# One-pass spreading of the gate rows of the first block, with a high and a low part, and the bound's exponential taken after the spread

## The reference

```
log_f = log_sigmoid(f_pre);  b = cumsum(log_f);  inter = b + m
d     = b[t] - b[s] + i[s]                  (s <= t, else -inf)
m_t   = max(inter, max_s d)
w     = exp(d - m_t);  qk = (q . k) * w
h     = num / max(|den|, exp(-m_t))
```

## Time and profile before

| | |
|---|---|
| median of 3 runs | 1403.32 us (1402.62 to 1403.69) |
| the profiled execution | 1404.49 us |
| its span, from the first to the last instruction | 1402.7 us |
| TensorE busy | 1386.1 us (99%) |
| VectorE busy | 1121.9 us (80%) |
| ScalarE busy | 848.6 us (61%) |
| mean granted clock of TensorE | 0.998 |

### The profile page before, as it was taken

One profiled execution on the slowest core, in us unless ns is written; L12 is line 12 of the kernel. 1 busy time (PEld: TensorE's weight loads), 2 busy tenths in 40 slices (PEclk: granted clock), 3 DMA queues, 4 the chain that ended last, 5 costly groups with the idle time before them and its releaser, 6 DMA issues.

```text
span 1402.7 us, 25844 instructions
## 1 busy us (share of the span) xinstructions
PE 1386.1 (99%) x10437; PEld 1306.4 (93%) x10437; DVE 1121.9 (80%) x1700; ACT 848.6 (61%) x1315; POOL 101.4 (7%) x157
## 2 busy tenths in 40 slices
PE   8999999999999999999999999999999999999998
PEld 8898888899889888899999999998999999999987
DVE  7898988889898889888788788767687787876653
ACT  6776776345876875446577575544464864755442
POOL 2000111100000011103100000000031000000000
PEclk9999999999999999999999999999999999999999
DMA  9643999986545999978955588887699556878662
GB/s 262 166 143 102 285 270 277 293 230 177 143 141 151 298 273 284 295 217 245 314 155 155 172 238 239 241 247 219 181 260 310 151 151 180 238 215 232 187 184 72
DMA packets 472981, 301.34 MB, mean 215 GB/s; under 512 B 15116, under 2 KB 454416, under 8 KB 472736
## 3 DMA queue, kind: packets, MB, share of 16 engines
q1 hardware_dynamic: 455344, 239.57, 61.2%
q0 software_dynamic: 16704, 58.29, 12.7%
q10 hardware_dynamic: 816, 1.84, 0.4%
HBM read 289.43 MB, written 1.05 MB: 207 GB/s over the span
## 4 chain that ended last, share of the span: by engine, by line
PE 79%; DVE 12%; ACT 3%; issue 3%; DMA 2%; SPq 0%; DVEq 0%; ACTq 0%
PE acc L2122 13%; PE acc L2123 13%; PE acc L2124 13%; PE mx L2139 8%; PE acc L2139 6%; PE mx L2140 4%; DVE w_lo L1186 4%; PE acc L2140 3%; DVE ada_acc L1276 2%; PE mx L2123 2%; PE mx L2124 2%; PE mx L2122 2%; DMA raw<-in_w_in 1%; ACT w_hi L596 1%; PE acc L2167 1%
## 5 line engine op out<-in xcount | busy, mean ns | idle before, releaser
L1186 DVE TENSOR_TENSOR w_lo<-raw,w_hi 128x1024 fp32r<-128x1024 f32 x450 | 542.5, 1220 | 126.6 <-ACT w_hi L596 124.6
L596 ACT ACTIVATE w_hi<-raw 128x1024 fp32r<-128x1024 f32 x450 | 464.5, 1052 | 130.3 <-DMA raw<-in_w_in 61.4
L2122 PE MATMUL acc<-h,w_hi 128*128 128x256 f32 (+1 forms) x1472 | 418.9, 285 | 2.9 <-DVE w_lo L1186 1.9
L2123 PE MATMUL acc<-h,w_hi 128*128 128x256 f32 (+1 forms) x1472 | 413.0, 281 | 0.0
L2124 PE MATMUL acc<-h,w_lo 128*128 128x256 f32 (+1 forms) x1472 | 411.8, 280 | 0.0
L2122 PEld LDWEIGHTS acc<-h,w_hi 128*128 128x128 f32 x1472 | 277.4, 188 | 8.1 <-DVE w_lo L1186 2.3
L2123 PEld LDWEIGHTS acc<-h,w_hi 128*128 128x128 f32 x1472 | 277.6, 189 | 1.4 <-issue 1.0
L2124 PEld LDWEIGHTS acc<-h,w_lo 128*128 128x128 f32 x1472 | 278.0, 189 | 0.0
L2139 PE MATMUL mx<-u,w_hi 128*128 128x512 f32 x756 | 264.4, 392 | 0.0
L2140 PE MATMUL mx<-u,w_lo 128*128 128x256 f32 x756 | 213.1, 282 | 0.0
L2139 PEld LDWEIGHTS mx<-u,w_hi 128*128 128x128 f32 x756 | 141.9, 188 | 29.2
(11 more groups left out here) (339 smaller groups left out, 2297.7 us busy)
## 6 DMA issues: line engine op xcount, KB each, us to landing
raw<-in_w_in SPq DMA_DIRECT2D x132, 512.0 KB, 4.1
ada<-in_w_ada POOLq DMA_DIRECT2D x96, 512.0 KB, 5.9
raw<-in_w_ffn_in SPq DMA_DIRECT2D x88, 512.0 KB, 4.1
raw<-in_w_up SPq DMA_DIRECT2D x64, 512.0 KB, 5.5
raw<-in_w_down SPq DMA_DIRECT2D x64, 512.0 KB, 5.9
raw<-in_w_out SPq DMA_DIRECT2D x32, 512.0 KB, 3.9
raw<-in_w_ffn_out SPq DMA_DIRECT2D x32, 512.0 KB, 4.1
raw<-in_w_ret_o SPq DMA_DIRECT2D x16, 512.0 KB, 4.1
```

The source lines that it names most:

```text
L596: nc.scalar.activation(w_hi[:, n % NS], raw[:, n % NS], ACT.Copy).then_inc(hi_ready, 1)
L1186: V.tensor_tensor(w_lo[:, n % NS], raw[:, n % NS], w_hi[:, n % NS].bitcast(F32), ALU.subtract).then_inc(lo_ready, 1)
L2122: mm(outp, w_hi[:, i % NS, k], rhs[:, k, 0], start=k == 0, stop=False)
L2123: mm(outp, w_hi[:, i % NS, k], rhs[:, k, 1], start=False, stop=False)
```

## The change

1. `g_M` is split into a high part (fp32r) on partitions 0 to 3 and a low part on partitions 32 to 35 of a zeroed tile `g_M2` of 36 rows. The spreading matmul has 36 rows, a selecting column that is repeated over the 128 outputs (`pick`), and one pass in fp32r; it sums both parts. All four heads are done after slab 9.
2. The bound: G is clipped before the exponential (to the logarithms of the old limits), split in the same way (`g_G2`), spread in one pass, and ScalarE takes exp(-2 x) as it reads the spread rows from the bank. `forget_exp` and `gates_clipped` are gone.
3. `sums(0)` moves into slab 10, after its third piece. `gate_columns` goes from behind slab 9 to behind slab 10.
4. VectorE: slab 8 is read out before the splitting; `w_lo` of slabs 13 and 14 follows the last tap instead of preceding it; 2 memsets at the start of a layer, 4 small copies at the program's start for `pick` and `pick_pairs`.
5. ScalarE: `spread_exp` is ahead of the convolution's silu.
6. The padding ahead of `u2` grows from 32 to 148 words a partition, beside the new tiles.

```diff
+            with ExitStack() as until_values:
+                g_M2 = sb("g_M2", [36, S], F32R, until_values)
+                g_G2 = sb("g_G2", [36, S], F32R, until_values)
...
-                def forget_exp():
-                    act.wait_ge(f_G, l + 1)
-                    nc.scalar.activation(g_E[:], g_G[:], ACT.Exp, scale=-2.0).then_inc(f_E, 1)
...
-                    nc.scalar.activation(ebc[:], mx[:, 0], ACT.Copy).then_inc(f_bcsb, 1)
+                    nc.scalar.activation(ebc[:], mx[:, 0], ACT.Exp, scale=-2.0).then_inc(f_bcsb, 1)
...
                 ahead(13)
-                forget_exp()
                 ahead(14)
                 head_square(0)
                 head_seed(0)
                 ahead(15)
+                spread_exp()
                 conv_silu()
                 spread_max()
-                spread_exp()
...
+                boot.done(V.tensor_copy(pick[0:32], con[0:32, K_ID:K_ID + 4]))
+                boot.done(V.tensor_copy(pick[32:36], con[32:36, K_ID + 32:K_ID + 36]))
+                boot.done(V.tensor_copy(pick_pairs[0:32], con[0:32, K_ID:K_ID + 4].unsqueeze(2).to_broadcast([32, 4, HD])))
+                boot.done(V.tensor_copy(pick_pairs[32:36], con[32:36, K_ID + 32:K_ID + 36].unsqueeze(2).to_broadcast([4, 4, HD])))
...
-                    V.tensor_tensor(g_G[:], g_F[:], g_M[:], ALU.add).then_inc(f_G, 1)
-                    dve.wait_ge(f_G, l + 1)
-
-                def gates_clipped():
-                    dve.wait_ge(f_E, l + 1)
-                    V.tensor_scalar(g_E[:], g_E[:], 1e30, 1e-33, ALU.min, ALU.max).then_inc(f_E2, 1)
+
+                def gate_parts():
+
+                    c.link(V.tensor_copy(g_M2[0:4], g_M[:]))
+                    V.tensor_tensor(g_M2[32:36], g_M[:], g_M2[0:4].bitcast(F32), ALU.subtract).then_inc(f_parts, 1)
+
+                def bound_parts():
+
+                    c.link(V.tensor_tensor(g_G[:], g_F[:], g_M[:], ALU.add))
+                    c.link(V.tensor_scalar(g_G[:], g_G[:], G_HIGH, G_LOW, ALU.min, ALU.max))
+                    c.link(V.tensor_copy(g_G2[0:4], g_G[:]))
+                    V.tensor_tensor(g_G2[32:36], g_G[:], g_G2[0:4].bitcast(F32), ALU.subtract).then_inc(f_parts, 1)
...
                 c.done(V.memset(ones4[:], 1.0))
+                c.done(V.memset(g_M2[:].bitcast(F32), 0.0))
+                c.done(V.memset(g_G2[:].bitcast(F32), 0.0))
...
                 def gate_rows(n):
-                    pe.wait_ge(s_con, 32)
-                    pe.wait_ge(f_M, l + 1)
+                    pe.wait_ge(f_parts, l * 2 + 1)
...
-                        ins = mm(mx[:, 1 + n, i * S:(i + 1) * S], con[0:4, K_SEL + h * P:K_SEL + (h + 1) * P], g_M[:],
+                        ins = mm(mx[:, 1 + n, i * S:(i + 1) * S], pick[:, h:h + 1].to_broadcast([36, P]), g_M2[:],
...
-                        ins = mm(mx[:, 0, n * S:(n + 1) * S], con[0:4, K_PAIR + n * P:K_PAIR + (n + 1) * P], g_E[:],
-                                 start=True, stop=True)
+                        ins = mm(mx[:, 0, n * S:(n + 1) * S], pick_pairs[:, 2 * n:2 * n + 2].rearrange("p h d -> p (h d)"),
+                                 g_G2[:], start=True, stop=True)
```

More of the change, by code:

```diff
@@ L16 @@
+import math
 from contextlib import ExitStack
@@ L37 @@
 BIG = 1e30
+G_LOW, G_HIGH = -0.5 * math.log(1e30), -0.5 * math.log(1e-33)
 A_PROJ, A_OUT, A_MLP = 23, 8, 64
@@ L250, in program @@
         ada_part = sb("ada_part", [P, 4])
+        pick = sb("pick", [36, 4], F32R)
+        pick_pairs = sb("pick_pairs", [36, 4, HD], F32R)
         few = sb("few", [P, 16])
@@ L253, in program @@
         wgrp = sb("wgrp", [P, LAYERS * 4, P])
-        sb("before_u2", [P, 32])
+        sb("before_u2", [P, 148])
         with ExitStack() as mlp:
@@ L387, in program @@
         cv_first = sem("cv_first"); cv_ready = sem("cv_ready"); cv_silu = sem("cv_silu")
-        f_abs = sem("f_abs"); f_ln = sem("f_ln"); f_M = sem("f_M"); f_G = sem("f_G"); f_E = sem("f_E"); f_E2 = sem("f_E2")
+        f_abs = sem("f_abs"); f_ln = sem("f_ln"); f_M = sem("f_M");
         f_bc = sem("f_bc"); f_bcsb = sem("f_bcsb"); f_uc = sem("f_uc"); f_ucsb = sem("f_ucsb")
-        f_exp = sem("f_exp"); ml_v = sem("ml_v"); ml_rs = sem("ml_rs")
+        f_parts = sem("f_parts"); f_exp = sem("f_exp"); ml_v = sem("ml_v"); ml_rs = sem("ml_rs")
         ml_s = sem("ml_s"); ml_arg = sem("ml_arg"); ml_w = sem("ml_w"); ml_p = sem("ml_p"); ml_nd = sem("ml_nd")
@@ L1444, in arguments @@
                         dve.wait_ge(s_con, 32)
-                    dve.wait_ge(f_bcsb, l * 3 + h // 2 + 1)
+                    dve.wait_ge(f_bcsb, l * 3 + h // 2 + 2)
                     if h >= 2:
@@ L1469, in ml_bounded @@
                     dve.wait_ge(ml_d, l + 1)
-                    dve.wait_ge(f_bcsb, l * 3 + 3)
+                    dve.wait_ge(f_bcsb, l * 3 + 1)
                     c.link(V.tensor_tensor(m_d, m_d, ebc[:], ALU.max))
@@ L1567, in _ @@
                 gate_maxima()
-                to_sbuf(7)
+                to_sbuf(7, 8)
+                gate_parts()
                 convolve(2)
-                gates_clipped()
-                to_sbuf(8)
+                bound_parts()
+                lo_upto(p0 + 12)
+                convolve(3)
                 lo_upto(p0 + 14)
-                convolve(3)
                 gate_negated()
@@ L2233, in project @@
                              before=(lambda k: pe.wait_ge(h_ready, l * 16 + k + 1)) if i == 0 else
-                             (lambda k: norm_sum(l * 2) if k == (4 if l else 7) else None) if i == 1 else None).then_inc(slab_used, 1)
+                             (lambda k: norm_sum(l * 2) if k == (4 if l else 7) else None) if i == 1 else
+                             (lambda k: sums(0) if k == 3 else None) if i == 10 else None).then_inc(slab_used, 1)
                 def gate_rows(n):
-                    pe.wait_ge(s_con, 32)
-                    pe.wait_ge(f_M, l + 1)
+                    pe.wait_ge(f_parts, l * 2 + 1)
                     for i in range(2):
                         h = 2 * n + i
-                        ins = mm(mx[:, 1 + n, i * S:(i + 1) * S], con[0:4, K_SEL + h * P:K_SEL + (h + 1) * P], g_M[:],
+                        ins = mm(mx[:, 1 + n, i * S:(i + 1) * S], pick[:, h:h + 1].to_broadcast([36, P]), g_M2[:],
                                  start=True, stop=True)
@@ L2250, in gate_columns @@
                         mm(mx[:, 3, 4 * t:4 * t + 4], g_u[:, t * P:(t + 1) * P], con[0:4, K_ID:K_ID + 4], start=True, stop=True)
[L2251 removed]
+                    pe.wait_ge(f_parts, l * 2 + 2)
                     for n in range(2):
[L2253 to L2254 removed]
+                        ins = mm(mx[:, 0, n * S:(n + 1) * S], pick_pairs[:, 2 * n:2 * n + 2].rearrange("p h d -> p (h d)"),
+                                 g_G2[:], start=True, stop=True)
                     ins.then_inc(f_uc, 1)
@@ L2396, in _ @@
                     rest_of_vectors()
-                project(3, 4, 5, 6, 7, 8)
+                project(3, 4, 5, 6, 7, 8, 9)
                 gate_rows(0)
-                project(9)
-                sums(0)
+                gate_rows(1)
+                project(10)
                 gate_columns()
-                project(10)
-                gate_rows(1)
                 project(11, 12)
+                pe.wait_ge(f_bcsb, l * 3 + 2)
+                ml_scores(0)
                 pe.wait_ge(f_bcsb, l * 3 + 3)
-                ml_scores(0)
-                pe.wait_ge(f_bcsb, l * 3 + 2)
                 values(0)
```

1 line of the change is left out of this document (removed).

## The result

The changed kernel takes 1405.89 us (median of 20 runs, 1403.65 to 1409.14) beside 1403.61 us (20 runs, 1402.09 to 1405.51) for the kernel before on the same chip: a ratio of 1.0013 [1.0007, 1.0019], 1.8 us more by the ratio (2.3 by the two medians), where 1 us less was forecast. A second measurement gave 1.0010 [1.0002, 1.0019]. Small as it is, the sign is wrong, and the time lies above the range.

The account below looks back on a forecast made before the run. TensorE, 99% busy, was taken as the bound, tied to a chain of VectorE, sync queue and copies. Gains kept, 0.1 + 0.8, about 1 us, took the profiled 1404.49 to 1403.5, median 1402.3; range 1399.5 to 1405.3.

Parts of the forecast that it names:

- The slack: First layer, before slab 12: TensorE could begin at 51.98 but does at 54.36, so 2.4 us to draw on.
- new waits at slab 12: TensorE waits for VectorE's reading of slab 9: 2.6 us in the first layer, 1.3 in the second.
- Rival 2: TensorE's saving counts in full in both layers, 2.8 + 2.5 = 5.3 us, so 1398.0; chance 12%.
- rival 3: Gate rows still cost 1.0 us and more; TensorE only waits less at slab 12, time within 0.3; inside the 45%.
- The padding: Moved padding ahead of u2: costed at nothing, since no row showed an address mattering.
- Rival 1: New waits lower the clock at slabs 12 and 13, 1.7 us each: 1403.9 (27%, first layer) or 1405.2 (8%, both).
- Step 1: Four start copies add 0.7 us to VectorE, carried to slab 9; VectorE's 2.1 us delay ends in idle before 60.24.
- The term of the memsets: Two memsets lie where VectorE waits for the norm's sum and cost nothing; without that cover, 0.4 us.
- Step 2: Result of sums(0), counted from slab 8's end: equally late in the first layer, 0.26 us later in the second.
- TensorE's sum: Small matmuls per layer: gate rows 0.47, sums(0) 1.17, gate_columns 0.92, together 2.56 instead of 5.08; saves 2.5 us.
- Step 3: VectorE's added less removed work: net +1.44 us a layer, range 1.2 to 1.7.
- the place that counts: Copies of pair 1 on the sync queue set the end; forecast 0.1 us earlier in the first layer, 0.8 in the second.

Follow-up runs that it names:

- sums_first: Changed kernel with sums(0) right behind slab 9, ahead of the gate rows, instead of inside slab 10; 1405.22 us, ratio to the kernel before 1.0005.
- start_twice: Changed kernel with its four start copies done twice at the same place; 1406.55 us, ratio to the kernel before 1.0025.
- sums_late: Changed kernel with sums(0) after slab 10's seventh piece instead of its third; 1406.64 us, ratio to the kernel before 1.0017.
- start_early: Changed kernel with the four start copies moved ahead of VectorE's first reading of the turned tokens; 1404.18 us, ratio to the kernel before 1.0001.
- sums_and_start: Changed kernel with the start copies early and sums(0) right behind slab 9; 1404.12 us, ratio to the kernel before 1.0001.
- start_only: Kernel before plus only the changed kernel's four start copies, memsets, new tiles and padding; 1406.39 us, ratio to the kernel before 1.0015.
- start_only_early: start_only with the four copies moved ahead of the first tokens, where VectorE is idle; 1404.41 us, ratio to the kernel before 1.0001.
- after: The changed kernel itself, first profile; 1405.89 us, ratio to the kernel before 1.0013.
- after_again: The changed kernel once more, unaltered, for a second profile; ratio to the kernel before 1.0010.
- before_again: The kernel before once more, unaltered, for a second profile; ratio to the kernel before 1.0001.
- read9_early: Changed kernel with VectorE reading out slab 9 right behind the bound's split, ahead of w_lo of slab 12; 1404.65 us, ratio to the kernel before 1.0005.
- pad_only: Kernel before with the padding ahead of u2 at 408 words instead of 32 (address 157056); 1412.93 us, ratio to the kernel before 1.0061.
- pad_32bytes: Kernel before with the padding ahead of u2 at 40 words instead of 32 (address 155584); 1405.8 us, ratio to the kernel before 1.0010.
- pad_same: Kernel before with u2 at the changed kernel's address (padding 416 words, address 157088); 1403.5 us, ratio to the kernel before 0.9994.

## Why the prediction was wrong

**What held.** The slack was used up as worked out: new waits at slab 12 of 2.33 and 1.07 us (forecast 2.6 and 1.3), put down to the reading of slab 9. Rival 2, the full saving, is out. The one-pass form is real: rival 3 in its strict form is out. The padding costs nothing.

**Rival 1, lower clock behind the new wait, had 35% and is real, but does not come in every execution.** Five profiles have a wait of 2.31 to 2.38 us at slab 12 of the first layer: the two of the changed kernel, sums_first, start_twice and sums_late. In the last two the clock fell behind it, in the other three it didn't. It fell neither behind the waits of 1.56 (start_early) and 1.25 us (sums_and_start) nor behind any in the second layer, and none of the ten other profiles shows a fall there. So both profiles of the changed kernel happen to be without it, and they can't say how often its other executions have it. The prediction had said as much: "the fall may come in some executions alone".

**Step 1 that failed: the start copies.** The term was 0.7 us, "VectorE has no idle time from there to slab 9, so it carries this along"; they take 1.0. The size is minor. I then let the delay die: "VectorE's delay of 2.1 us ends in its idle times before 60.24", and for the first layer "that chain ends there whatever TensorE does, so of the 0.24 I keep 0.1". But that chain is made of VectorE and of ScalarE behind it. A delay of VectorE moves the readings of slabs 6 to 8, and with them slab 8, `sums(0)` and the chain. start_only against start_only_early shows it without any other part of the change: 1.02 us at the scan, 1.07 at the copies of pair 1. In the changed kernel with the clock at 0.57 at the start, it is less: start_early takes the copies out of the way and `rv` comes 0.25, the copies of pair 1 0.27 earlier.

The term of the memsets failed with it: "cost nothing" holds with a clock of 0.57 at the start; with 1.00 they put slab 2 off by 0.41 us.

**Step 2 that failed: "The result of `sums(0)` ... comes after 2.80 + 0.47 + 1.05: the same."** Before, `rv` starts 45.98 - 12.08 = 33.90 behind slab 0, after 47.20 - 12.73 = 34.47: 0.57 later. 0.39 of it are the gate rows: TensorE needs 0.86 us for them, not 0.47. Slab matmuls stand at 44.11 ahead of them and at 44.98 and 45.20 behind (below), so 1.09 us less two steps of 0.117; the pass itself is as short as forecast, and the rest lies in the changes to it and back, which I had allowed for fp32 alone. Rival 3 named this cost, but said that TensorE would then only wait less at slab 12; it forgot that `sums(0)` stands behind the rows. Slab 8 itself ends 0.21 later (its last matmul stands 28.34 and 28.55 behind slab 0), by the start copies; 0.03 of gain, as forecast, goes off. The other two terms of TensorE's sum were off as well, one each way: `sums(0)` alone put 0.86 into the stream, not 1.17, `gate_columns` 1.16, not 0.92; all three make 2.88, not 2.56. TensorE's timeline around the gate rows:

```profile
44.11 0.28 PE L2139 MATMUL acc<-h,w_lo 128*128 128x256 f32 x1
...
44.98 0.39 PE L2137 MATMUL acc<-h,w_hi 128*128 128x256 f32 x1
45.20 0.28 PE L2138 MATMUL acc<-h,w_hi 128*128 128x256 f32 x1
```

In the second layer `rv` is 0.66 to 0.89 later where 0.26 was forecast, and the copies gain 0.24 to 0.48 instead of 0.8. So what was saved on TensorE lies behind the one small matmul that the chain waited for, and that one came later; sums_late puts the price at 1 us on the copies for each us of `rv`.

**Step 3, mis-sized:** VectorE's net is 1.65 a layer, not 1.44 (subtraction 0.41 + 0.03 each, where I had 0.34).

**The sum with these.** 0.5 us lost and 0.24 to 0.48 gained make 0 to 0.3 us, not 1.8. By the times, taking the start copies out of VectorE's way takes the loss away: from 1.0013 and 1.0010 to 1.0001 in the changed kernel, from 1.0015 to 1.0001 in the kernel before with them. How these four copies come to cost that much is not traced to its end; two reasons for more than the table are on record.

The first is the clock at the start. Both profiles of the changed kernel had it at 0.57 from 13 to 17 us. Then TensorE is late by itself in the first layer, and covers the memsets and part of VectorE's delay. With the clock at 1.00 the kernel before has the copies at 59.98. No profile shows the changed kernel so, but two estimates agree. From sums_first: it has them at 60.55 with `sums(0)` earlier, which is worth 0.67 (61.21 - 60.27, less 0.27 for the start copies), so 61.2. From start_twice: 63.10 less the 0.88 of VectorE's waits behind the fall and 1.07 for the second set, so 61.15. That is an estimate of 1.2 us lost in such an execution, against 0.5 in the others; nine of seventeen profiles had the low clock. The mean of both, about 0.8 less 0.35 for the second layer, is 0.5 of the 1.8.

The second is rival 1 in executions without a profile. Their mean granted clock is on record to three places. The 32 runs of the changed kernel that are listed with it have 0.9975 on the mean (4 of them at 0.996), the 127 of the kernel before 0.9981 (2 at 0.996). By profile, sums_late with both falls has 0.996, start_twice with the one behind slab 12 alone 0.997, after and after_again with the one at the start alone 0.997 and 0.998, and before_again with neither 0.999. The variants go the same way: start_twice, sums_late and sums_first 0.9975 to 0.9977, start_early and sums_and_start, whose wait at slab 12 is shorter, 0.9984. The difference of 0.0006 is 0.9 us of 1404, an estimate and a bound, since it counts only where TensorE's lateness reaches the end, and it overlaps with the first reason. Against it: within the 32 runs the time hardly goes with the clock (1406.0 us on the mean at 0.996, 1405.4 at 0.999), and read9_early, without that wait but with 1.9 us at the next, has 0.9972. So it is a reason that fits, not one that is shown.

What is left is open: what lies between the copies and the next layer differs between twins (251.67 and 250.88 us from the copies of pair 1 to the second layer's norm sum in the changed kernel's two profiles), and I could not tie that to the code.

That the copies of pair 1 are the place that counts was only half right too: sums_late's time grew by about half of what it lost there in the two layers.

## What to carry to other kernels

When the engine that is 99% busy is made faster, ask which of its small instructions starts the longest chain on the others, and whether that one comes earlier or later; a saving placed around it is worth nothing. Work for an engine in the chain can cost its full time even once, at the start of the program, if it stands in a stretch without idle time, and nothing in an idle gap earlier: look for that gap first. Read a difference of 1 us from landmarks of two profiles each, not from one. And an event that comes in some executions only, as the fall of the clock here, is not ruled out by two profiles without it: look in the variants' profiles too.

## What the runs showed of the hardware

- The start of the program meets the clock in two ways, the same kernel too. Windows 13 to 17 us of before_again and of after_again:

```profile
13.00:17.00 4.00, 3.56 (x31) 3.36 (x30) 3.90 (x8) 3.32 (x6) 0.00 (x0) 1.00 0.91 172
```

```profile
13.00:17.00 4.00, 4.00 (x23) 4.00 (x22) 3.90 (x8) 3.65 (x6) 0.00 (x0) 0.57 0.82 134
```

  Before slab 0 TensorE had been idle for 1.33 us in the first and 2.21 in the second. In the nine profiles with a clock of 0.57 to 0.60 this was 1.84 to 2.58 us, in the eight with 1.00 it was 1.33 to 1.86. Amid dense matmuls, a wait of 2.31 to 2.38 us was followed by a fall in two of five profiles (to 0.57 over 56 to 60 us in start_twice, to 0.51 over 54 to 56 in sums_late), and waits of 1.56 us and less at slab 12 by none.
- The Trainium skill ("TensorE: Matmul & The Clock Gate", Part 1) lets the monitor run free of the kernel, so that twins may meet it differently; the two profiles of the kernel before do (0.57 in rows 9, 1.00 here).
- Where a matmul's moving operand starts in memory can cost it 1 to 2%: 399 (pad_only) and 397 ns (pad_32bytes) against 392 (pad_same) for 512 columns; 4.8, 3.5 and 0 us over all matmuls that read it.
- An fp32r matmul of 36 rows amid fp32r matmuls of 128 rows costs more than its pass: four took 0.86 us instead of 0.47. The starts have gaps of about 0.1 us more at the change to them and back; whether the rows, the repeated column or the waits for a semaphore there cause them was not separated.
